# Attention masks gathered between the high and the cross products of a key tile

## What is computed

```python
for blk in range(seq // B_BLOCK):
    s0 = blk * B_BLOCK; s1 = s0 + B_BLOCK
    logits = (jnp.einsum('bhqd,bhkd->bhqk', q[:, :, s0:s1], k[:, :, :s1]).astype(jnp.float32)
              + log_f_cum[:, :, s0:s1, None] - log_f_cum[:, :, None, :s1])
    causal = jnp.arange(s0, s1)[:, None] >= jnp.arange(s1)[None, :]
    p = jax.nn.softmax(jnp.where(causal, logits, -jnp.inf), axis=-1)
    outs.append(jnp.einsum('bhqk,bhkd->bhqd', p.astype(v.dtype), v[:, :, :s1]))
```

## Time and profile before

| | |
|---|---|
| median of 3 runs | 3468.64 us (3466.01 to 3476.93) |
| the profiled execution | 3470.49 us |
| its span (first to last instruction) | 3468.9 us |
| attention within the span, first rough to last value product | about 2417 to 3244 us |
| PE / DVE / ACT / POOL busy over the span | 90% / 51% / 35% / 30% |

### The profile page before, as it was taken

How to read it: one execution, slowest core, us unless ns; L and a number is a source line. 1 busy time by engine, 2 the same in 40 slices (tenths; PEclk the granted TensorE clock), 3 DMA queues, 4 the chain that set the end, 5 groups by cost and what they waited for, 6 DMA issues and landing times. The chain is left out here.

```text
span 3468.9 us, 40912 instructions
## 1 busy us (share of the span) xinstructions
PE 3128.4 (90%) x15182; PEld 2334.1 (67%) x15182; DVE 1764.7 (51%) x2659; ACT 1227.0 (35%) x2102; POOL 1040.8 (30%) x764
## 2 busy tenths in 40 slices
PE   5888789999978997995999959997899999999798
PEld 4666567888857886884888848885455555555476
DVE  4544444557555665554221142211687787778433
ACT  4344445544414554224110041110244444445311
POOL 0478860123215551110000000001254445455210
PEclk8999899999989998997999989998699999999899
DMA  5233431576736663555432154412736334330333
GB/s 208 69 127 99 128 103 50 166 228 195 222 104 216 202 210 131 177 165 165 121 97 61 49 159 114 118 73 77 164 70 144 94 78 104 83 86 13 113 127 121
DMA packets 270101, 436.35 MB, mean 126 GB/s; under 512 B 73214, under 2 KB 170118, under 8 KB 259612
## 3 DMA queue, kind: packets, MB, share of 16 engines
q1 hardware_dynamic: 230812, 332.18, 32.9%
q0 software_dynamic: 23008, 86.08, 7.9%
q10 hardware_dynamic: 16112, 15.86, 1.6%
HBM read 283.10 MB, written 150.82 MB: 125 GB/s over the span
## 5 line engine op out<-in xcount | busy, mean ns | idle before, releaser
L2039 DVE TENSOR_REDUCE at_partial<-at_rough 128x1 f32<-128x512 f32 (+3 forms) x640 | 370.4, 605 | 180.7 <-PE at_rough L1948 136.3
L2127 ACT ACTIVATE at_probs<-at_logits 128x512 f32<-128x512 f32 (+3 forms) x640 | 331.0, 534 | 362.0 <-PE at_logits L1963 309.5
L174 PE MATMUL pa_y<-pa_h_high,pa_w_high 128*128 128x512 f32 x1056 | 422.1, 400 | 7.4 <-ACT pa_acc L840 5.5
L176 PE MATMUL pa_y<-pa_h_high,pa_w_low 128*128 128x512 f32 x1056 | 412.4, 391 | 0.0
L175 PE MATMUL pa_y<-pa_h_low,pa_w_high 128*128 128x512 f32 x1056 | 412.4, 391 | 0.0
L1873 POOL TENSOR_TENSOR at_sum_g<-at_sum_g,at_probs 128x512 f32<-128x512 f32 (+3 forms) x256 | 304.2, 1188 | 236.1 <-ACT at_probs L2127 221.6
L1960 PE MATMUL at_logits<-at_Q,at_K 67*128 67x512 f32 (+3 forms) x640 | 265.2, 414 | 26.2 <-DMA at_Q<-at_minus_top 19.6
L1974 PE MATMUL at_o<-at_probs,at_V 128*64 128x512 f32 (+3 forms) x1280 | 270.6, 544 | 0.0
L1963 PE MATMUL at_logits<-at_Q,at_K 128*128 128x512 f32 (+3 forms) x640 | 256.1, 400 | 0.0
L1948 PE MATMUL at_rough<-at_K,at_Q 66*128 66x512 f32 (+3 forms) x640 | 242.1, 390 | 15.5 <-DMA at_K<-s_Fp 14.8
L174 PE MATMUL pk_y<-pk_h_high,pk_w_high 128*128 128x512 f32 x544 | 218.3, 401 | 30.5 <-POOL pk_ident L99 27.7
(11 more groups left out here) (346 smaller groups left out, 5631.5 us busy)
## 6 DMA issues: line engine op xcount, KB each, us to landing
at_Q<-s_Q SPq DMA_DIRECT2D x96, 256.0 KB, 6.7
s_qkv<-pa_sil POOLq DMA_DIRECT2D x16, 1024.0 KB, 6.6
pa_sil<-s_qkv SPq DMA_DIRECT2D x16, 1024.0 KB
dr_kv<-s_qkv SPq DMA_DIRECT2D x16, 1024.0 KB
s_K<-pk_parts SPq DMA_DIRECT2D x32, 512.0 KB, 8.0
s_Q<-pb_parts SPq DMA_DIRECT2D x32, 512.0 KB, 8.0
at_K<-s_K SPq DMA_DIRECT2D x32, 512.0 KB, 5.6
pa_wraw<-in_a_w_in_dram ACTq DMA_DIRECT2D x15, 1024.0 KB
```

The lines of the kernel that those rows point to most:

```text
L174: nc.tensor.matmul(out, w_high[:, k], h_high[:, k], start=k == 0, stop=False)
L176: ins = nc.tensor.matmul(out, w_low[:, k], h_high[:, k], start=False, stop=k == KC - 1)
L2039: reduced.done(v.tensor_reduce(partial[:, u % 2, h * NQ + sub, grp:grp + 1], rough[:, j % 3, 0:width], AX.X, ALU.max))
L2127: probs_ok.done(a.activation(probs[:, R % 2, t, h, off:BLK], logits[:, l % 3, off:BLK], ACT.Exp))
```

## The change

Within a round, PE's program for a key tile becomes: high product of head 0, (for t = 0) high product of head 1, this tile's half of the rough products, (for t = 1) high product of head 1, the masks of the last two rough products, the masks of both heads, the cross product of head 0, the cross product of head 1. The waits and their targets are the same. Two rough products whose masks stand together may be signalled by one increment of two. DVE's list of reductions is cut at the same half; for rounds of four it is the same as before.

```diff
-                if grp == qb:
-                    ins = nc.tensor.matmul(bank[:, sub * P:width], ident_b[:, :], mask_q[:, :], start=False, stop=True)
-                rough_ok.done(ins)
...
-                    part = -(-len(items) // 4)
+                    half = -(-len(items) // 2)
                     for t, kb, off in tiles(R):
+                        mine = items[t * half:(t + 1) * half]
+                        high_logits(R, t, kb, off, 0)
+                        if not t:
+                            high_logits(R, t, kb, off, 1)
+                        for j in mine[:-2]:
+                            ins = rough_logits(j)
+                            rough_done([j], mask_rough(j) if on_diagonal(j) else ins)
+                        pending = []
+                        for j in mine[-2:]:
+                            ins = rough_logits(j)
+                            if on_diagonal(j) or pending:
+                                pending.append(j)
+                            else:
+                                rough_done([j], ins)
+                        if t:
+                            high_logits(R, t, kb, off, 1)
+                        while pending:
+                            ins = mask_rough(pending[0])
+                            upto = next((n for n in range(1, len(pending)) if on_diagonal(pending[n])), len(pending))
+                            rough_done(pending[:upto], ins)
+                            pending = pending[upto:]
                         for h in range(2):
-                            exact_logits(R, t, kb, off, h)
-                            for j in items[(2 * t + h) * part:(2 * t + h + 1) * part]:
-                                if j == FIRST:
-                                    pe.wait_ge(rows_q, 2)
-                                rough_logits(j)
+                            mask_logits(R, t, kb, off, h)
+                        for h in range(2):
+                            cross_logits(R, t, kb, off, h)
...
-                    half = 2 * -(-len(items) // 4)
+                    half = -(-len(items) // 2)
```

More of the change, by code:

```diff
@@ L1938, in rough_logits @@
             def rough_logits(j):
+                if j == FIRST:
+                    pe.wait_ge(rows_q, 2)
                 u, h, sub, grp = ITEMS[j]
@@ L1999, in _ @@
                 rough_logits(j)
+                rough_done([j], mask_rough(j))
             pe.wait_ge(consts, 1)
```

27 lines of the change are left out of this document (20 added, 7 removed).

## The result

The change makes the kernel slower: 3487.36 us (median of 10 runs, 3479.55 to 3489.08) against 3467.09 us (median of 10 runs beside them, 3465.02 to 3476.93), a ratio of 1.0054 [1.0045, 1.0062]. The forecast was 3491.1 us, slower by 0.65%.

The account below looks back on a forecast made before the run. PE was taken to bound attention. Masks -7.2, short products +2.5, the chain through the exponential +35.2 and replaced waits -8.0 gave +22.5 us, from the median 3468.64 to 3491.1 us; range 3473 to 3506.

Parts of the forecast that it names:

- The bound: In attention from 2500 us PE is busy 99 of each 100 us, so only its work or waits change the time.
- The chain: A round's last high product waits for its first exponential: 1.27 us against five matmuls of 1.175 us; +35.2 us in all.
- what is replaced: PE's earlier 19 waits for exponentials at high products, with late weights, were taken as counted anew: -8.0 us.
- table of rounds: Chain loss at last high products, added up by kinds of round and widths of their rough products: +35.2 us.
- The masks: The 512 mask products on PE, standing in 276 stretches instead of alone: 48.4 us against 55.6, -7.2 us.
- A follower: A mask directly behind another mask on PE; 236 of them, taken at 0.065 us each against 0.12 for a lone one.
- Short products: 128-column f32 products followed by another f32 product, whose weights come late: 57 pairs before, 105 after, +2.5 us.
- The signs: Predicted trace marks: PE's exponential waits up from 6 to 20 us or more, 0.34 us last high products, masks 0.05-0.08 us apart.
- The short lag: Rival: a round's first exponential also starts 0.43 us behind its cross product, not 0.52; sum +9.4, 3478 us; chance 0.17.
- Covered: Rival: the last high product finds its bank free, so masks alone count: -12.7, 3456 us; chance 0.08.
- Followers as dear as lone masks: Rival: a mask behind a mask costs 0.12 us, not 0.065: +13.0, 3504 us; chance 0.11.
- DVE as the bound: Rival: DVE's sums sit out POOL's, lengthening its round to 5.6 us: +72, 3563 us; chance 0.03.

Follow-up runs that it names:

- e2: The changed kernel, but of a round's four rough products one stands in t = 0 and three in t = 1: 3468.32 us, ratio 1.0006.
- e4: The changed kernel, but from round 8 on a round's first exponential covers only the right half of its columns: 3461.46 us, ratio 0.9987.
- e11: The changed kernel, but ACT passes the first exponential's three long fulfilled waits again ahead of the third: that starts 0.512 us behind its cross product, not 0.432.
- e3: The changed kernel's order of products, but each mask stands right behind its own product: 3478.42 us, ratio 1.0038 to the kernel before.
- e5: The changed kernel, but off the diagonal the masks of t = 1's rough products stand ahead of the last high product: 3475.4 us, ratio 1.0017.

## Why the prediction was right

**The bound**: right. PE sets attention's time before and after, DVE in neither.

**The chain.** The mechanism was right and it decides, by e2 and e4. Each link came out as written: 0.51, 0.60, 0.05 and 0.115 late where 0.52, 0.60, 0.05 and 0.105 were forecast. Its term, 35.2 - 8.0 = +27.2 us, was too small: +31.1 was measured (14.6 us before, 45.7 after). Two of its parts were off, in opposite directions.

**The step that failed is "what is replaced", -8.0.** It supposed that the waits in the earlier trace rows would be counted anew in the table of rounds. They were not replaced. In 31 rounds from the sixth on the last high product lost over 0.1 us before, 14.3 us in all. After the change it loses 20.7 there, 6.4 more, where the table adds 7.1 for these rounds: the new loss came on top of the old one. In the other 124 rounds it lost 0.4 us before and 25.1 after, for which the table has 27.9. The price of the old waits was too low too, since it rested on PE's 19 waits alone: 35 high products waited, and in the 16 that only the row of the weight load lists, the weights came late as well. What the prediction says of the 17.3 us themselves is right: most of it is time behind the matmul ahead, in the round above 0.27 us of idle weight load for a start that was 0.04 late.

**The table of 35.2** was too large by about 4 us. Most of that is in the rounds of 256 and 128 columns, for which it adds 9.5 us where 6.3 were measured.

The old waits in part stand where ACT is late, in rounds in which it also issues two transfers. One such round, after:

```profile
2607.80 1.21 ACTq L2143 DMA_DIRECT2D at_Q<-at_minus_top  x2
...
2609.20 1.08 ACT L2165 ACTIVATE at_probs<-at_logits 128x512 f32<-128x512 f32 x2 [1.43 <-PE at_logits L1980]
...
2609.85 0.50 PE L1969 MATMUL at_logits<-at_Q,at_K 67*128 67x512 f32 x1 [0.46 <-ACT at_probs L2165]
```

ACT was busy issuing its two transfers up to 2609.01, the exponential began at 2609.20, and PE idled for 0.46 us (0.35 in the earlier trace rows, the same round before). The exponential stands 2.03 us behind the round's first high product in both kernels, but the last high product is due 2.07 us behind it instead of 2.14.

**The masks.** Right: -8.8 us with the waits behind them taken out, where -7.2 was forecast. (The row of the table says -12.4, of which 3.6 are waits of the chain.) A lone mask costs 0.12 as read. A follower costs 0.055 to 0.056, not 0.065. Four masks in a stretch show it, 0.21 us for all and 0.08 behind them at the next product, 0.29 = 0.12 + 3 x 0.056:

```profile
2603.62 0.29 PE L1956 MATMUL at_rough<-at_mask_q,at_ident_b 128*128 128x128 bf16 x2
2603.75 0.27 PE L1974 MATMUL at_logits<-at_mask_k,at_ident_b 128*128 128x128 bf16 x2
2603.83 0.48 PE L1980 MATMUL at_logits<-at_Q,at_K 128*128 128x256 f32 x2
2604.15 0.22 PE L1969 MATMUL at_logits<-at_Q,at_K 67*128 67x128 f32 x1
```

With that price the sum is 276 x 0.12 + 236 x 0.055 = 46.1, against 55.6 that is -9.5 us. It covers all of attention, the table only the rounds from the sixth on. There stand 471 masks in 248 stretches after, 248 x 0.12 + 223 x 0.055 = 42.0, where 42.3 were measured, and 472 before, 104 of them ahead of value products or partition sums, 368 x 0.12 + 104 x 0.065 = 50.9, where 51.1 were measured. So the prices of the prediction fit both kernels. The rate that the Trainium skill gives for a sustained stream (TensorE: Matmul & The Clock Gate, Back-to-back issue gap, about 81 ns a pair) did not show in these stretches of two to four: 56 ns.

**Masks and chain together**: +22.3 us measured, +20.0 forecast.

**Short products**: +2.4 measured, +2.5 forecast.

**What the sum left out**: rough products lost 4.6 us less than before and other places 2.4. The waits for DVE at rough products didn't enter the sum. Nearly all of the 6.4 us before are of that kind, such as this one, where the cross product ahead holds PE from 2613.91 to 2614.33, 0.42 us instead of 0.235, and the rough product behind the wait then 0.17 us instead of 0.067:

```profile
2614.33 0.19 PEld L1948 LDWEIGHTS at_rough<-at_K,at_Q 66*128 66x128 f32 x1 [0.46 <-DVE at_partial L2039]
```

After the change rough products lose 1.8 us. That they do because DVE got faster is argued, not shown; of the other 2.4 us no cause is known.

**The sum**: +22.5 forecast; +20.3 by the medians, 3487.36 - 3467.09; in the traces +17.7 from the sixth round on. That it came so near is in part luck: the chain was 3.9 us too small (the -8.0 too much, the table 4 too large), the masks 1.6 too dear, and 7.0 us of gains at rough products and elsewhere were in no term. The round at 2622.80 grew from 4.89 to 5.10 us, by 0.21. I had written about 0.1, but its own terms give 0.15 for the chain and 0.055 for a mask that no longer stands ahead of value products.

**The signs.** The waits that PE's own row counts rose from 6.0 to 14.4 us, not to 20 or more as written; the loss that they stand for did, since most of it is late weights and starts of under 0.15 us, which that row doesn't list. The place (second half of a round), the 0.35 us for the product and the distances in a stretch came as written. Rounds on the diagonal came out about even: 5.27 to 5.23 us and 4.16 to 4.18.

**The rivals.** The short lag is out: 0.51 us was measured, and e11 shows why it stays, though the reason that the forecast leaned on (idle time) was the wrong one. Covered is out by the waits, 35 to 130. Followers as dear as lone masks is out, 0.056. DVE as the bound is out, its sums became shorter on average. What no rival said, and e3 showed, is that the masks themselves were part of the cover.

## What to carry to other kernels

Before instructions are gathered to save their overhead, ask what they were hiding: between a bank's producer and its next writer every instruction is cover, and what is taken out there comes back as a wait, here 31.1 us at one product against 8.8 us saved on masks. Before such a move count the links of the chain (issue to activation 0.51, activation 0.60, release 0.05, weights loaded late 0.11) against the matmuls in between, and change the order of rounds one class at a time, but measure neighbours together, since a round can pass lateness on to the next one through a reader that is behind. A wait can be listed at the weight load, at its matmul, or at both: don't add the rows, count the products that waited, and read what they cost from the distances between starts.

## What the runs showed of the hardware

**Waits that cost though they are fulfilled.** Three wait instructions ahead of an activation make it start 0.08 us later after its last releaser (e11: 0.432 to 0.512, 0.512 to 0.593). How the 0.08 divides over the three was not tried.

**Two sums and who starts first.** DVE's busy time fell from 79 to 68 us in 100 with the same reductions and sums to do. Its sum of the exponentials, the group of the kernel after from 2500 us on (count, busy us, mean ns) against 1064 ns in the earlier trace rows:

```profile
L2100 DVE TENSOR_TENSOR at_sum_v<-at_sum_v,at_probs 128x512 f32<-128x512 f32 x165 | 121.3, 735 | 22.6 <-ACT at_probs L2165 21.6
```

POOL's sums stayed at 1410 ns (1412 before). The time lines of a round, first before, with DVE and POOL:

```profile
2625.13 1.67 DVE L2062 TENSOR_TENSOR at_sum_v<-at_sum_v,at_probs 128x512 f32<-128x512 f32 x1
```

```profile
2624.96 2.96 POOL L1873 TENSOR_TENSOR at_sum_g<-at_sum_g,at_probs 128x512 f32<-128x512 f32 x2 [1.39 <-ACT at_probs L2127]
```

and then after:

```profile
2625.47 0.68 DVE L2100 TENSOR_TENSOR at_sum_v<-at_sum_v,at_probs 128x512 f32<-128x512 f32 x1
```

```profile
2625.97 1.32 POOL L1873 TENSOR_TENSOR at_sum_g<-at_sum_g,at_probs 128x512 f32<-128x512 f32 x1 [2.11 <-ACT at_probs L2165]
```

Behind a POOL sum that began 0.17 us earlier DVE's takes 1.67 us; with a start of 0.5 us ahead of POOL's it takes 0.68. Of 188 sums of 512 columns 80 took 0.6 to 0.7 us before and 137 after. 41 before and 118 after began ahead of the POOL sum with which they overlap, and each of these took 0.68 to 0.69 us; of those that began behind one, some took up to 1.8 us. This agrees with the Trainium skill, SBUF — State Buffer, Who interferes with whom, that of two such instructions the first goes first. No run here changed the starts alone, so the cause is argued and not shown. The gain on DVE moved no bound. (Its sums of 384 columns went the other way, 652 to 983 ns.)

**The high product behind a mask and behind a wait.** Both draw it out by about 0.1 us (0.08 and 0.11), and they don't add (e5: 0.33 us with both, against 0.35 with a wait alone).
